# Sixteen tokens moved from fetched expert rows to the dense expert products, and a ring of four instead of six

## What is computed

```python
h = rmsnorm(x, norm_g)                              # 256 tokens x 1024
q = (h @ w_query).reshape(T, 8, 2, 128)             # 8 heads, two halves
s = einsum('thpd,hpnd->thpn', q, sub_keys)          # 128 scores per half
vals, idx = top_k(s, 16)                            # top 16 of each half
cand = vals[:, :, 0, :, None] + vals[:, :, 1, None, :]
top_s, pos = top_k(cand, 16)                        # 16 experts of 128*128 per head
gates = softmax(top_s)
act = gelu(einsum('td,ted->te', h, u_table[experts]))     # 128 experts per token
out = einsum('te,ted->td', gates * act, v_table[experts])
```

## Time and profile before

| | us |
|---|---|
| median of three executions | 1664.42 |
| lowest and highest | 1657.94, 1670.57 |
| the profiled execution, its own time | 1666.97 |
| its span, first to last instruction | 1665.2 |
| TensorE busy (matmul) | 1592.1 |
| VectorE busy | 1087.6 |
| GpSimd busy | 459.4 |
| ScalarE busy | 296.3 |
| moved by the stream's queue | 321.43 MB |
| moved by GpSimd's queue | 204.60 MB |

### The profile page before, as it was taken

The page is one execution under the profiler, slowest core; times in us unless marked ns, Lnnn a source line. Parts: engine busy times, 40 slices in busy tenths (PEclk is TensorE's granted clock), DMA queues, the critical chain, the costliest instruction groups (busy, mean ns, idle before and its releaser), DMA issues.

```text
span 1665.2 us, 30651 instructions
## 1 busy us (share of the span) xinstructions
PE 1592.1 (96%) x11542; PEld 1461.7 (88%) x11542; DVE 1087.6 (65%) x2293; ACT 296.3 (18%) x632; POOL 459.4 (28%) x457
## 2 busy tenths in 40 slices
PE   8999999999999999999999999989999999999999
PEld 6788998899989998988977789989999899988888
DVE  5588779668846874444278777796787469644442
ACT  5485300100000000000057752001000000000000
POOL 0002024443432453333000020243434324433330
PEclk9999999999999999999999999999999999999999
DMA  7546479999999999999754364899999999999994
GB/s 245 162 144 195 152 264 392 403 379 384 400 398 349 372 406 391 401 396 386 257 176 139 110 202 142 281 402 393 393 379 381 408 345 391 408 385 397 395 404 167
DMA packets 149837, 531.82 MB, mean 319 GB/s; under 512 B 17712, under 2 KB 20992, under 8 KB 149376
## 3 DMA queue, kind: packets, MB, share of 16 engines
q1 hardware_dynamic: 88416, 321.43, 51.4%
q0 software_dynamic: 56672, 204.60, 32.3%
q10 hardware_dynamic: 4672, 4.81, 1.1%
HBM read 527.41 MB, written 1.06 MB: 317 GB/s over the span
## 4 chain that ended last, share of the span: by engine, by line
PE 68%; DMA 26%; issue 2%; DVE 2%; ACT 1%; SPq 0%; ACTq 0%; DVEq 0%; another core or an unknown queue 0%
PE ps L1853 26%; DMA raw<-stream 25%; PE ps L1793 21%; PE ps L1609 4%; PE ps L1624 3%; PE ps L1626 3%; PE ps L1625 3%; PE ps L1607 2%; PE ps L1804 1%; PE ps L1781 1%; PE ps L1744 1%; PE ps L1606 1%; PE ps L1934 0%; PE ps L1964 0%; ACT big L596 0%
## 5 line engine op out<-in xcount | busy, mean ns | idle before, releaser
L1853 PE MATMUL ps<-big,raw 128*128 (+1 forms) x4096 | 593.3, 303 | 24.6 <-DMA raw<-stream 16.9
L1793 PE MATMUL ps<-big,raw 128*128 128x160 f32 x4096 | 587.3, 302 | 29.1 <-DMA raw<-stream 23.8
L1853 PEld LDWEIGHTS ps<-big,raw 128*128 128x128 f32 x4096 | 560.7, 190 | 53.8 <-issue 43.3
L1793 PEld LDWEIGHTS ps<-big,raw 128*128 128x128 f32 x4096 | 559.9, 190 | 51.8 <-DMA raw<-stream 26.7
L1365 DVE SCALAR_TENSOR_TENSOR big<-big,own_act 128x1024 f32<-128x1024 f32 x192 | 246.4, 1283 | 214.9 <-PE ps L1853 202.9
L546 POOL DMA_INDIRECT big<-v_rows,own x192 | 203.8, 1062 | 366.8 <-DVE big L1365 333.1
L1260 DVE SCALAR_TENSOR_TENSOR big<-big 128x1024 f32<-128x1024 f32 x192 | 231.1, 1226 | 107.6 <-PE ps L1793 77.2
L546 POOL DMA_INDIRECT big<-u_rows,own x192 | 210.1, 1094 | 312.5 <-DVE big L1260 282.8
L579 ACT ACTIVATE wh<-raw 128x1024 fp32r<-128x1024 f32 x97 | 102.1, 1056 | 334.8 <-DMA raw<-stream 301.2
L778 ACT ACTIVATE big<-ps 128x320 f32<-128x320 f32 x128 | 55.9, 437 | 566.8 <-PE ps L1793 513.5
L903 DVE TENSOR_TENSOR wl<-raw,wh 128x1024 fp32r<-128x1024 f32 x97 | 121.6, 1264 | 48.4 <-ACT wh L579 26.1
(11 more groups left out here) (250 smaller groups left out, 1109.7 us busy)
## 6 DMA issues: line engine op xcount, KB each, us to landing
raw<-stream SPq DMA_DIRECT2D x609, 512.0 KB
big<-u_rows,own POOLq DMA_INDIRECT x192
big<-v_rows,own POOLq DMA_INDIRECT x192
big<-keys ACTq DMA_DIRECT2D x2, 1024.0 KB, 7.4
big<-row_copy ACTq DMA_DIRECT2D x6, 256.0 KB, 5.5
x<-x_in SPq DMA_DIRECT2D x1, 1024.0 KB, 5.6
big<-big POOLq DMA_DIRECT2D x4, 256.0 KB, 3.4
big<-big POOLq DMA_DIRECT2D x8, 128.0 KB, 3.8
```

Of the source, the lines that this page charges most:

```text
L1793: i = pe.matmul(ps[:, r % 4, 0:N], w[:, kd, :], h32[:, kd, :], start=(kd == 0), stop=(kd == KD - 1))
L1853: i = pe.matmul(ps[:, c // 2, c % 2 * N:(c % 2 + 1) * N], w[:, c, :], g, start=(fresh_bank and c % 2 == 0), stop=last, skip_group_check=True)
```

## The change

Sixteen tokens go from the fetched to the dense way: 176 dense, 80 fetched. `FETCHES` becomes 80, the number of one-hot groups 22. The second group of fetched tokens has 16 tokens, so its rows are copied 8 times instead of 4, and the same holds for the expert numbers and the gates. The ring of fetched rows is four deep. The areas of `own_h`, `h32` and `fetched` move up, since `G` is larger.

```diff
-GT2 = 32
+GT2 = 16
 N = S - GT - GT2
 REST = N - P
 FETCHES = SLOTS * (GT + GT2) // P
-FETCH_RING = 6
+FETCH_RING = 4
...
-        own_h = [area(22528, D), area(23552, D)]
+        own_h = [area(26624, D), area(27648, D)]
         own_gain = area(18432, D)
         own_out = [area(24576, D), area(25600, D)]
-        h32 = area(20480, KD, N)
-        fetched = area(26624, FETCH_RING, D)
+        h32 = area(22528, KD, N)
+        fetched = area(28672, FETCH_RING, D)
```

## The result

The changed kernel takes **1715.07 us** (median of 4, 1711.31 to 1718.35) against 1666.11 us for the kernel before (median of 4): ratio 1.0302, 95% interval 1.0266 to 1.0339. It is 49 us slower; 20 were forecast, and 1715 lies above the range.

What follows compares the result with a forecast made beforehand. Transfers bound the row stretches, TensorE the rest; afterwards TensorE. Dearer dense tokens +113.8, fewer fetches -110.9, remaining stalls 2 x 8.5: +20 us on the median 1664.4, so 1684 us (+1.2%), range 1668 to 1706.

Steps and rivals of the forecast that it cites:

- What bounds the kernel: Dense stages: transfers set the pace in row stretches before; after the change the bound moves to TensorE.
- The price of 16 columns and of one more call a half: Dense stages: a unit takes 2.388 us, two more `weights` calls cost 2.1 us a layer; 113.8 us in all.
- What the fetches cost before: Dense stages of both layers: 110.9 us over TensorE's floor of 580.9 us a layer, all that fewer fetches can give back.
- The rest R: Dense stages after the change: stalls left over TensorE's floor, 8.5 us a layer, forecast between 6 and 15.
- the traffic of the sum: Row stages after the change: 376 GB/s asked for at TensorE's pace, under the 395 carried.
- The upper end of R: Dense stages: rows always under way, 130 units outside the one-hots coming at 2.56 us, 22 us of stalls a layer.
- Rival 2: Dense stages: transfers stay the bound, stalls of 16 to 22 us a layer, +35 to +47 us, 1699 to 1711; chance 0.13.
- the limit of about 358 GB/s: Memory share of a core by the skill's rule: row-stage units 2.51 us, stalls about 17 us a layer; 395 GB/s kept instead.
- The range: Whole kernel: 1668 to 1706 us, from the low end of the wash to the middle of the case that transfers stay the bound.
- The ring, VectorE, the routing: Four row slots not late, VectorE's 41 us less and 10 more worth nothing, routing results covered by 14 us.
- VectorE's waits for rows: Routing: 3 waits of 1 to 2 us for fetched rows, none outside the routing.
- The top-16 result: Routing: comes at about 288 us instead of 282.3, needed at 302 by unit 44's gelu.

Runs made afterwards that it cites:

- experiment 2: Changed kernel (176 dense tokens) with each weight unit loaded in two halves, reloaded as each half is used; 1678.96 us, ratio 1.0127 to the kernel before.
- short-row run: Kernel before (160 dense tokens) with row fetches of 64 columns instead of 1024: 1563.01 us; the same cut in the changed kernel (176): 1676.72 us.

## Why the prediction was wrong

- **What bounds the kernel.** Right. Before, the transfers: with short rows the dense stages fall to their floor, 111 us less. After, TensorE: 80% of the chain, 92% with the halves of experiment 2.
- **The price of 16 columns and of one more call a half.** Right: 2.387 us a unit against 2.388, and 113.4 to 113.7 us measured against 113.8.
- **What the fetches cost before.** The 110.9 us over the floor were counted right in the trace, and the short-row run shows the floor itself: 580.9 us in both layers.
- **The rest R: this step failed.** "Between the ends I go by the stretch nearest in traffic", 2 to 3% lost, 8.5 us a layer. R was 21.1 and 19.6. The size of this one term is the whole error between the profiled executions: 2 x (20.4 - 8.5) = 24 of the 24 us between forecast (+20) and measurement (+44). The reason is that traffic was the wrong likeness. Experiment 2 carries 374 GB/s, the traffic of the sum, through the row stretch and loses nothing there, so no rate explains the loss. What decides is the time to a unit's last part (7.1 us in the median, and often more) against the lead (7.16 us). The stretches I took for nearest have a call of `weights` in every fourth unit, 1.05 us in which TensorE uses no weights: the lead is up to 8.2 us and most delays are caught up. That part of `down` lost 1% after the change; the row stretch, with no such pause after its first units, lost 6%. I had the unit's landing times of 7 to 8 us in hand and used them for the ring of rows, where they did not matter, instead of laying them against three units of stream.
- **The upper end of R** (22 us, stream at half share all the time) was right as a bound. R came to 93% of it by another mechanism: units are not 2.56 us apart but 2.39, with single stops of up to 1.6 us. Rival 2 had this outcome (+35 to +47, chance 0.13) with the wrong reason. So had the limit of about 358 GB/s in the Trainium skill (DMA: Bandwidth & Descriptors, Specifications), by which the prediction put R at 17. The kernel after carried 350 and looks like it, but 374 GB/s without loss in experiment 2 shows that no such limit was met.
- **The range.** It ended in the middle of rival 2 because I gave that rival 0.13. The landing times, laid against the lead, would have spoken for an R of that size.
- **The ring, VectorE, the routing.** Right, nothing of it is on the path. But VectorE's waits for rows were counted low: three of 1 to 2 us were forecast for the routing, and the two layers together show 16, 30.3 us in all, one of 8.5 us. The top-16 result came at 284.9 + 0.4 us (forecast 288, before 282.3), the gates at 310.1 (forecast 312), with no wait behind them.

## What to carry to other kernels

Where one engine consumes what a ring delivers, two tests stand side by side: bytes per unit of time against what the queues carry, and the time from issue to the landing of the *last part* against the lead of the ring (buffers less one, times the consumer's pace). Passing the first says nothing of the second; a chain whose DMA pieces are as long as the lead, while the queues are not full, tells of the second. (In the kernel before the pieces are as long, 6.8 to 8.5 us, but the share is 1.01.) Here finer release of the buffers bought back most of the loss where the queues had room, and cost 1.2% where they were full.

## What was not expected of the hardware

- Beside a second queue of row fetches the 16 parts of one 512 KB transfer land over 2.2 to 2.3 us (4.8 to 7.1 us after the buffer was free); with nothing beside it they land within 0.5 to 0.8 us (3.2 to 3.7 or 4.0). Rows of half the bytes narrow it to 1.8 to 1.9 us and bring the end forward by 1.4 us. Half of the loss goes when the rows are neighbours and fetched by a plain copy.
- The same edit (pieces of 2 KB a packet, half a unit more lead) took 29 to 36 us off with the queues at 374 GB/s, and added some 20 us with the queues full.
- With four row buffers instead of six at 160 tokens VectorE waited 110.9 us for rows over the run (80.2 + 30.7), and the kernel's time did not change within 0.3%.
